# Layer 2's output projection starts inside the attention's last two rounds

## What is computed

```python
q, k, v = odd_project(h_lat, w_in)                 # 16 query heads, 2 key/value heads, width 64
y = window_gqa_sink(q, k, v, qc, kc, vc, sink)     # 128-token window on each side, 256 context keys, a sink
y = y @ w_out                                      # 512 x 1024 times 1024 x 1024
x_lat = layer_norm(DN_ALPHA * x_lat + m_lat[2] * y, ln_g, ln_b)
f = conv_ffn(modulate(x_lat, m_lat[3], m_lat[4]), ...)
x_lat = layer_norm(DN_ALPHA * x_lat + m_lat[5] * f, ...)
```

## Time and profile before

| | us |
|---|---|
| median of 3 runs | 2430.82 (2429.23 to 2434.2) |
| the profiled execution | 2431.32 |
| its span, first to last instruction | 2429.5 |
| TensorE busy, share of the span | 96% |
| layer 2's output projection on TensorE | 2000.1 to 2047.5 |

### The profile page before, as it was taken

The page is one execution under the profiler, slowest core; times in us unless marked ns, Lnnn a source line. Parts: engine busy times, 40 slices in busy tenths (PEclk is TensorE's granted clock), DMA queues, the critical chain, the costliest instruction groups (busy, mean ns, idle before and its releaser), DMA issues.

```text
span 2429.5 us, 33136 instructions
## 1 busy us (share of the span) xinstructions
PE 2324.1 (96%) x13146; PEld 1885.6 (78%) x13146; DVE 1549.6 (64%) x2465; ACT 949.2 (39%) x1768; POOL 349.5 (14%) x455
## 2 busy tenths in 40 slices
PE   6999899999999899999999999999999999999998
PEld 3876567888887788777878888888877778888886
DVE  3648686566767652566879885656474767765457
ACT  4426464322222421566342232332352774423333
POOL 0110100000022210101000313223112120101131
PEclk8999999999999999999999999999998999999999
DMA  6330024744544312110422333234122103432321
GB/s 263 118 108 25 19 88 163 250 170 156 167 136 156 110 56 80 68 62 9 166 66 94 131 122 110 96 108 139 44 79 78 37 14 143 150 111 87 104 87 70
DMA packets 79178, 257.58 MB, mean 106 GB/s; under 512 B 5680, under 2 KB 10416, under 8 KB 70576
## 3 DMA queue, kind: packets, MB, share of 16 engines
q1 hardware_dynamic: 65024, 205.01, 24.5%
q0 software_dynamic: 12704, 46.14, 5.5%
q10 hardware_dynamic: 1296, 4.30, 0.4%
HBM read 246.00 MB, written 9.44 MB: 105 GB/s over the span
## 4 chain that ended last, share of the span: by engine, by line
PE 81%; DVE 9%; ACT 3%; issue 3%; DMA 2%; POOL 1%; SPq 1%; POOLq 0%; DVEq 0%; ACTq 0%
PE PS L1288 11%; PE PS L1289 11%; PE PS L1290 11%; PE PS L1359 5%; PE PS L1360 5%; PE PS L1361 5%; PE PS L1165 4%; PE PS L1204 3%; PE PS L1184 3%; PE PS L996 3%; PE PS L999 3%; PE PS L997 3%; PE PS L1053 1%; PE PS L1257 1%; PE PS L1260 1%
## 5 line engine op out<-in xcount | busy, mean ns | idle before, releaser
L1288 PE MATMUL PS<-HH,WH 128*128 128x512 f32 (+1 forms) x1088 | 420.8, 387 | 9.2 <-DVE TMP L2578 4.6
L1289 PE MATMUL PS<-HL,WH 128*128 128x512 f32 (+1 forms) x1088 | 417.2, 383 | 0.0
L1290 PE MATMUL PS<-HH,WL 128*128 128x512 f32 (+1 forms) x1088 | 417.1, 383 | 0.0
L2771 ACT ACTIVATE WH<-STG 128x1024 fp32r<-128x1024 f32 (+1 forms) x202 | 196.7, 1022 | 272.6 <-PE PS L1361 236.1
L2365 DVE TENSOR_TENSOR WL<-STG,WH 128x1024 fp32r<-128x1024 f32 (+1 forms) x202 | 241.8, 1238 | 37.0 <-ACT WH L2771 36.9
L1288 PEld LDWEIGHTS PS<-HH,WH 128*128 128x128 f32 x1088 | 204.6, 188 | 53.7 <-issue 5.7
L1359 PE MATMUL PS<-WH,AH 128*128 128x512 f32 x600 | 235.8, 393 | 7.4 <-DVE WL L2365 3.4
L1898 DVE SCALAR_TENSOR_TENSOR ACC<-ADAW,CS,ACC 128x1024 f32<-128x1024 f32 x168 | 225.4, 1377 | 21.8 <-PE PS L999 14.4
L1290 PEld LDWEIGHTS PS<-HH,WL 128*128 128x128 f32 x1088 | 204.6, 188 | 40.1
L1289 PEld LDWEIGHTS PS<-HL,WH 128*128 128x128 f32 x1088 | 204.7, 188 | 39.9 <-issue 1.0
L1360 PE MATMUL PS<-WL,AH 128*128 128x512 f32 x600 | 234.5, 391 | 0.0
(11 more groups left out here) (273 smaller groups left out, 4451.6 us busy)
## 6 DMA issues: line engine op xcount, KB each, us to landing
STG<-in_w_up SPq DMA_DIRECT2D x66, 1024.0 KB, 6.3
ADAW<-in_w_ada SPq DMA_DIRECT2D x96, 512.0 KB, 3.8
STG<-in_w_down SPq DMA_DIRECT2D x20, 1024.0 KB, 5.1
ADAW<-in_w_ada POOLq DMA_DIRECT2D x32, 512.0 KB, 4.0
STG<-in_w_ffn_out SPq DMA_DIRECT2D x10, 1024.0 KB, 6.3
STG<-in_ev_w_in SPq DMA_DIRECT2D x8, 1024.0 KB, 5.1
STG<-in_w_in SPq DMA_DIRECT2D x6, 1024.0 KB, 7.0
spill<-X POOLq DMA_DIRECT2D x10, 512.0 KB, 5.1
```

What stands on the lines that cost most here:

```text
L1288: e.matmul(out, h_, hh, start=c == 0, stop=False)
L1289: e.matmul(out, h_, hl, start=False, stop=False)
L1290: return e.matmul(out, l_, hh, start=False, stop=c == 7)
L2771: return e.activation(dst, src, ACT.Copy)
```

## The change

- ScalarE copies the high parts of tile 2 in round 31 and of tile 3 in round 32 of the attention (`out_high_early`), behind its own work of the round. These copies wait until item 31's maxima are taken (their destination overlaps the window masks) and until the columns that they read are in X.
- DVE makes the low parts of tile 2 behind its work of round 32, and of tile 3 behind that of round 33, which is its very last result.
- TensorE does the first twelve products of (0,0) at the end of round 32, ahead of item 31's inverse transpose and result. After round 33 it drains and signs `("att", 2)`, then does the other twelve. It no longer waits for the other engines' signatures in layer 2.
- GpSimd's and SP's programs are not edited; ScalarE and DVE have only tile 4's parts left to make after the signatures.

```diff
@@ -678,6 +678,16 @@
 
     n = len(WOUT_TT[L])
     return [[x for x in range(3, n) if out_place_before(x) == i] for i in range(n)]
+
+
+def out_high_early(L, p):
+
+    return {(2, 31): [(0, 0), (0, 1)], (2, 32): [(1, 0), (1, 1)]}.get((L, p), [])
+
+
+def out_early(L):
+
+    return 2 if L == 2 else 0
 
 
 def out_split(L, p):
@@ -1218,6 +1228,14 @@
             if 1 <= i <= N:
                 for u in turning_order(items[i - 1])[1:]:
                     turn(i - 1, u)
+            if L == 2 and i >= N:
+                if i == N:
+                    rot["set"], rot["n"] = list(range(8)), 0
+                    first_bank = take(("wo", 2, LAT[0], 0))
+                    out_products(2, 0, 0, first_bank, range(4))
+                else:
+                    e.drain().then_inc(*k.pe_end.up(("att", 2)))
+                    out_products(2, 0, 0, first_bank, range(4, 8))
 
     def pairs(a, items, bg):
 
@@ -1242,24 +1260,30 @@
         a.out_pair(len(items) - 1, 5, items[-1]["v"])
         a.close()
 
+    def out_products(L, i, n, b, cs):
+        tt = WOUT_TT[L][i]
+        xh, xl = k.out_parts(L, i)
+        for c in cs:
+            wh, wl = k.out_weights(L, n, c // 4)
+            x = slice(c * P, (c + 1) * P)
+            w.wait_ge(*k.ac_xh((L, tt, c // 4)))
+            w.wait_ge(*k.dv_wolo((L, n, c // 4, c % 4 // 2)))
+            e.matmul(PS[:, b, :], xh[:, x], wh[:, c % 4, :], start=c == 0, stop=False)
+            e.matmul(PS[:, b, :], xh[:, x], wl[:, c % 4, :], start=False, stop=False)
+            w.wait_ge(*k.dv_xl((L, tt, c // 4)))
+            m = e.matmul(PS[:, b, :], xl[:, x], wh[:, c % 4, :], start=False, stop=c == 7)
+        if cs[-1] == 7:
+            m.then_inc(*k.pe_wout.up((L, tt) if n else (L, tt, 0)))
+            freed[b] = [k.dv_yg(("wo", L, tt, n))]
+
     def w_out(L, bg):
-        for x in (k.dv_end, k.ac_end, k.pl_end):
-            w.wait_ge(*x(("att", L)))
+        if L < 2:
+            for x in (k.dv_end, k.ac_end, k.pl_end):
+                w.wait_ge(*x(("att", L)))
         for i, n in out_order(L):
             tt = WOUT_TT[L][i]
-            xh, xl = k.out_parts(L, i)
-            b = take(("wo", L, tt, n))
-            for c in range(8):
-                wh, wl = k.out_weights(L, n, c // 4)
-                x = slice(c * P, (c + 1) * P)
-                w.wait_ge(*k.ac_xh((L, tt, c // 4)))
-                w.wait_ge(*k.dv_wolo((L, n, c // 4, c % 4 // 2)))
-                e.matmul(PS[:, b, :], xh[:, x], wh[:, c % 4, :], start=c == 0, stop=False)
-                e.matmul(PS[:, b, :], xh[:, x], wl[:, c % 4, :], start=False, stop=False)
-                w.wait_ge(*k.dv_xl((L, tt, c // 4)))
-                m = e.matmul(PS[:, b, :], xl[:, x], wh[:, c % 4, :], start=False, stop=c == 7)
-            m.then_inc(*k.pe_wout.up((L, tt) if n else (L, tt, 0)))
-            freed[b] = [k.dv_yg(("wo", L, tt, n))]
+            if (L, i, n) != (2, 0, 0):
+                out_products(L, i, n, take(("wo", L, tt, n)), range(8))
             if n:
                 step(bg, ((3, 2, 2, 0) if L == 0 else (3, 1, 1, 1, 0, 0))[i])
                 if i == len(WOUT_TT[L]) - 2:
@@ -1542,8 +1566,9 @@
         rot["set"], rot["n"] = [6, 7], 0
         scores_ready(L)
         woven_pairs(L, items_of(k, L))
-        rot["set"], rot["n"] = list(range(8)), 0
-        e.drain().then_inc(*k.pe_end.up(("att", L)))
+        if L == 1:
+            rot["set"], rot["n"] = list(range(8)), 0
+            e.drain().then_inc(*k.pe_end.up(("att", L)))
         bg = ada(10, 16) if L == 1 else ada(16, 17)
         w_out(L, bg if L == 1 else iter(()))
         e.drain().then_inc(*k.pe_end.up(("wo", L)))
@@ -2280,6 +2305,8 @@
                 copies(i - 1)
             if out_split(L, i - 1):
                 out_weights_low(L, 0, *out_split(L, i - 1))
+            for x, h in out_high_early(L, i - 1):
+                out_low(L, x, h)
 
     def layer_norm(stage, L, tt, ready):
         key, x = (stage, L, tt), k.x(tt)
@@ -2364,6 +2391,12 @@
             w.wait_ge(*k.ac_whi((L, pi, i)))
             e.tensor_tensor(lo[:, x], raw[:, x], hi[:, x].bitcast(F32), ALU.subtract).then_inc(*k.dv_wlo.up((L, pi, i)))
 
+    def out_low(L, i, h):
+        xh, xl = k.out_parts(L, i)
+        tt, x = WOUT_TT[L][i], slice(h * 512, h * 512 + 512)
+        w.wait_ge(*k.ac_xh((L, tt, h)))
+        e.tensor_tensor(xl[:, x], k.x(tt)[:, x], xh[:, x].bitcast(F32), ALU.subtract).then_inc(*k.dv_xl.up((L, tt, h)))
+
     def w_out(L, bg):
         last = len(WOUT_TT[L]) - 1
 
@@ -2374,12 +2407,8 @@
                 layer_norm("a", L, tt, [k.dv_x(("wo", L, tt, 1))])
 
         def low(i):
-            xh, xl = k.out_parts(L, i)
-            tt = WOUT_TT[L][i]
             for h in range(2):
-                x = slice(h * 512, h * 512 + 512)
-                w.wait_ge(*k.ac_xh((L, tt, h)))
-                e.tensor_tensor(xl[:, x], k.x(tt)[:, x], xh[:, x].bitcast(F32), ALU.subtract).then_inc(*k.dv_xl.up((L, tt, h)))
+                out_low(L, i, h)
 
         def regain(i):
 
@@ -2394,7 +2423,7 @@
 
         for s in k.ends(("att", L)):
             w.wait_ge(*s)
-        for i in range(3):
+        for i in range(out_early(L), 3):
             low(i)
         for h in range(2):
             for i in range(2):
@@ -3037,6 +3066,8 @@
                     sink(i)
             if out_split(L, i):
                 out_weights_high(L, 0, *out_split(L, i))
+            for x, h in out_high_early(L, i):
+                out_high(L, x, h)
 
     def turn_mid(L, f):
 
@@ -3086,6 +3117,14 @@
                 w.wait_ge(*k.dv_wg((pi, i)))
             copy(hi[:, x], raw[:, x]).then_inc(*k.ac_whi.up((L, pi, i)))
 
+    def out_high(L, i, h):
+        xh, _ = k.out_parts(L, i)
+        tt, x = WOUT_TT[L][i], slice(h * 512, h * 512 + 512)
+        if i < out_early(L):
+            w.wait_ge(*k.dv_max((L, 31, 1)))
+            w.wait_ge(*k.dv_out((L, 4 * (4 * h + 3) + (3, 2, 4, 5).index(tt))))
+        copy(xh[:, x], k.x(tt)[:, x]).then_inc(*k.ac_xh.up((L, tt, h)))
+
     def w_out(L):
         last = len(WOUT_TT[L]) - 1
 
@@ -3097,17 +3136,14 @@
                 layer_norm("a", L, tt)
 
         def high(i):
-            xh, _ = k.out_parts(L, i)
-            tt = WOUT_TT[L][i]
             if i >= 3:
                 w.wait_ge(*k.pe_wout((L, WOUT_TT[L][out_place_before(i)])))
             for h in range(2):
-                x = slice(h * 512, h * 512 + 512)
-                copy(xh[:, x], k.x(tt)[:, x]).then_inc(*k.ac_xh.up((L, tt, h)))
+                out_high(L, i, h)
 
         for s in k.ends(("att", L)):
             w.wait_ge(*s)
-        for i in range(3):
+        for i in range(out_early(L), 3):
             high(i)
         for h in range(2):
             for i in range(2):
```

## The result

The changed kernel takes 2438.38 us (median of 18 runs, 2433.76 to 2445.36), the kernel before in the same comparison 2430.93 (18 runs). The ratio is 1.0032, with a 95% interval of 1.0022 to 1.0041: 7.5 us slower, 5 to 10 by the interval. The forecast was 2439.1.

What follows compares the result with a forecast made beforehand. The prediction took the stage to be bound by GpSimd's reads and DVE's work, not TensorE. Signature 4.8, queues 3.2 and clock 0.3 summed to 8.3 us, giving 2439.1 us (+0.34%), range 2433.5 to 2443.5.

Steps and rivals of the forecast that it cites:

- What bounds the stage: Output projection: GpSimd's reads of the old residue and then DVE's work end the stage, not TensorE, despite its busy time.
- The wait for the low part and the late result: Attention's end: TensorE idles about 1.5 us before its third product; item 31's result ends 3.6 us later.
- The signature: DVE's sign-off of the attention: late result 3.6 plus tile 3's low parts 1.2 delay it and GpSimd's issues 4.8 us.
- SP's loads: SP's first 1 MB load moves 2.75 us later, so 2.1 us earlier in relation to GpSimd's reads.
- The queues: DMA: SP's loads slow GpSimd's reads of the old residue by 3.2 us more; bounds nothing to 5.3.
- The rival with an even share: DMA queues: reads keep pace or share evenly, only the 4.8 us signature delay counts; 2435.6 to 2436.6 us, chance 0.17.
- The clock: TensorE at tile 5's products: a gap of some 8 us may halve the clock, costing 0.3 us; bounds 0 to 1.5.
- Rival C: Attention's end: TensorE's clock halves before the ten products, adding 3 us ahead of DVE's sign-off; 2442 us, chance 0.13.
- TensorE's earlier stream: TensorE reaches `turn_mid` 2.3 us earlier but gains nothing, waiting there for tile 3's norm, 8 us later than before.
- The sum: Whole stage: 4.8 for the late sign-off, 3.2 for slowed reads, 0.3 for the clock, together 8.3 us.

Runs made afterwards that it cites:

- 4: Changed kernel with all 24 products of (0,0) ahead of item 31's result in place of 12: one run, 2443.69 us; stage 87.2 us.
- 5: Changed kernel with the parts for the first twelve products made early, in rounds 16 and 17: ratio to before 1.0037, stage 81.3 us.
- 1: Changed kernel with SP's first feed-forward load held until tile 3's old residue has landed: ratio to before 1.0010, stage 79.9 us.
- before again: The kernel before, unchanged, run as a kernel of its own: ratio to before 0.9999, stage 76.1 us.
- 2: The kernel before with only SP's first feed-forward load held until tile 3's old residue has landed: ratio 0.9986, stage 76.2 us.
- 8: Changed kernel, SP held, reads before gain loads, six early-prepared products ahead of item 31's result, tile 3's low parts after the signature: ratio to before 0.9993.
- 3: Changed kernel with item 31's result and signature before all 24 products, tile 3's low parts behind DVE's signature: ratio to before 1.0014, stage 78.9 us.
- 7: Changed kernel with result and signature first, SP's load after the reads, GpSimd's first two reads before gain and bias loads: ratio to before 0.9993.
- 9: Changed kernel, twelve products kept ahead, SP's load after the reads, GpSimd's first two reads before gain and bias loads: ratio to before 0.9998.
- 6: Changed kernel with result and signature before all products and SP's first load after the reads: ratio to before 1.0003, stage 74.1 us.

## Why the prediction was right, by its steps

- **What bounds the stage.** Right. The chain still runs over GpSimd's reads and DVE. Taking SP's loads away from the reads brought 4.4 us, which a stage bound by TensorE could not do.
- **The wait for the low part and the late result.** Predicted 1.5 us of idleness and 3.6 us for the end of the result, measured 1.52 and 3.7. Numbers 4 and 5 moved it both ways, by 2.7 and 1.8.
- **The signature.** Predicted 4.8, measured 4.9 at GpSimd's first issue (14.78 less 9.88).
- **SP's loads.** Predicted 2.75 later, measured 2.66.
- **The queues.** Predicted 3.2 more between GpSimd's first issue and tile 3's regain, measured 19.05 less 15.97, 3.1. That SP's loads slow the reads was shown by 1. The rival with an even share misread how the queues share: they took turns by packets, not by bytes (see the last section), and SP's packets are about twice as large. The sum took the landing of tile 3's read as the only gate; tile 2's read, 3.7 us later than before relative to the first issue, and DVE's 2.4 us on it are nearly as late, and with SP's loads gone they are the gate. In the size of the forecast this made no difference.
- **The clock.** Predicted 0.3 in the stage. It fell in TensorE's long wait, as expected, and made the transposes behind the wait slower, but cost the stage nothing: from tile 4's residue sum to its end it was 31.3 us in both kernels. In 1 it cost 1.1. Rival C, the half clock ahead of the result, did not happen in any of the profiles with products there.
- **TensorE's earlier stream.** Right. Its products ahead of the transposes end 42.6 us after the scores of item 31 (predicted 42.2, before 44.5), and then it waits 1.2 us for tile 2's norm and 7.2 for tile 3's, so the 1.9 us are lost.
- **The sum.** 8.3 forecast, 8.0 in the stage, 7.5 in the median. Each of the two large terms came out within 0.1 us by itself, so the total is not two errors that cancel. For the time behind the stage the prediction put nothing.

What stays open: behind the stage the profiles are of two kinds, 363.4 to 363.7 us (before, before again, numbers 1, 2, 8) and 364.8 to 365.0 (changed, numbers 3 to 7 and 9). In the longer ones the clock falls once more, for 3.4 us, at the first feed-forward products of 512 columns, behind a wait of 2.5 us that all twelve profiles have. It fell there in seven of the nine profiles with early parts and in none of the three without. Whether the change makes this more likely cannot be said from one profile each; number 1, with the changed order, did not have it. The median does not decide it: 8.0 from the stage alone and 9.6 with it both lie in the interval, 5 to 10. The intervals of the table reach about 2.5 us to either side, and the times confirm none of the gains in the stage that numbers 6 to 9 have over the kernel before.

## What to carry to other kernels

Before work is put ahead of an engine's last result, count who is queued behind that result: here it was the signature that lets the next stage's reads start, and 2.3 us to gain on TensorE were paid for with 8 on the path of the reads. A load that nobody needs soon, and that the same edit brings nearer to the needed reads (here by 2.2 us), takes a share of the DMA engines from them; delaying it, and issuing the needed reads first, made the stage shorter than it had been at the start, though the times do not confirm a gain. Work moved early is free only in as much idle time as is there: six products whose parts were ready fitted, twelve did not.

## What the runs showed of the hardware beyond that

- Two DMA queues shared by packets and not by bytes. With both busy q0 moved 0.154 to 0.171 MB/us and q1 0.246 to 0.274. The packets are nearly as many on both: 271 and 229 in the earlier trace rows, 542 and 481 in the changed kernel. But q1's are larger: 1.74 MB in 229 packets are 7.6 KB each, q0's 0.98 MB in 271 are 3.6 KB each. "DMA: Bandwidth & Descriptors" of the Trainium skill (queues, rings and completion order) lets each DMA engine go round between the queues a packet at a time; the trace agrees, if the profile's packets are the ones meant.
- SP's data began some time after its issue, and how long hung on GpSimd's queue. Where that still had 1.6 to 3.5 MB to move, SP's first packet came 3.4 to 3.9 us after the issue (before: 2005.96 to 2009.42); in numbers 1, 2 and 6, where it had 0.5 MB or less left, 1.0 us.
- The half clock of TensorE costs by where it falls. In number 3 TensorE waited 3.5 us ahead of the transposes and the clock fell within the wait; from tile 4's residue sum on the stage took 31.3 us, as before. In number 1 it waited 3.1 us and the clock fell 1.8 us behind the wait, on tile 5's products; there it took 32.4. "TensorE: Matmul & The Clock Gate" of the Trainium skill (what is actually happening) sets the clock by recent busy time, and these runs agree in that it fell after waits, but not after every wait of the same length.
- A single profile's span is no measure of a change of this size: identical code ahead of the stage took between 1984.5 and 1994.2 us.
